# The low parts of nearly all weight units are added by accumulating transfers from HBM instead of being subtracted on GpSimd

## The chip, the cores and the metric

The kernel runs on one core of a Trainium2 chip. The metric is the device time in microseconds (us) of one execution, from its first to its last instruction. TensorE is PE, its weight loads PEld, VectorE is DVE, ScalarE is ACT, GpSimd is POOL, and SyncE is SP.

## The reference, cut to what matters

One inference step of a decoder trunk of two layers runs for 512 prompt tokens and 8 x 4 sample tokens, 544 in all, with a width of 1024 and everything in fp32. Each layer is:

```
u  = rms_norm(h, norm_mix) @ w_in                  # 25 column blocks of 128
h += concat[SSD, retention, GLA, RG-LRU](u) @ w_out # 8 column blocks
hn = rms_norm(h, norm_ffn)
h += (silu(hn @ w_gate) * (hn @ w_up)) @ w_down    # inner width 2816 = 22 blocks
```

and one last RMSNorm follows. The four mixers are recurrences in chunks with states of their own. The change touches none of them, only the way in which the weights of these products reach TensorE.

## The kernel before, in words

All weights are packed on the host into **units** of 128 partitions x 8 tiles x 128 columns, 512 KB each, 101 in a layer and 202 in all. A layer's units are, in order: 25 of w_in (numbers 0 to 24 in the layer, the mixer stage), 8 of w_out (25 to 32), then the FFN in groups: 16 gate and up units and 8 down units (33 to 56), the same again (57 to 80), and a last group of 6 blocks, REST, with 12 gate and up units (81 to 92) and 8 down units (93 to 100). A down unit of REST has only 6 tiles in use; its transfers move 8.

Each fp32 product is made of three passes over values that are split into a high and a low part: `wh*xh + wh*xl + wl*xh`. `unit_half` issues them for one unit and half of the tokens: 8 tiles x 3 matmuls of 272 columns, 48 matmuls for the two halves, 36 in a down unit of REST. `wh` is the weight rounded to fp32r by an ACT copy of `raw` (L420). `wl = raw - wh`, the **rest**, is made in one of two ways, and `added(n)` says which for unit n:

- subtracted: POOL computes `raw - wh` on 128 x 1024 (L391) as soon as `wh` is there (semaphore `lo_done`);
- added: ACT writes `wl = -raw` (L419, semaphore `negated`) ahead of `wh` (L420), and POOL issues a transfer of the unit from HBM that adds into `wl` (L397, semaphore `lo_added`). Since the destination is rounded to fp32r on both writes, what remains is the low part. ACT and the second read of the unit from HBM take the place of POOL's subtraction.

`raw`, `wh` and `wl` are rings of three slots. Unit n can be prepared only when TensorE has finished unit n-3 (`dense_done`, waited for in `hi_ahead`), so ACT's and POOL's work and the transfer must fit into the time of units n-2 and n-1. SP loads `raw` of unit n+3 (L375) when slot n is free: for an added unit after ACT's `wh` of unit n, for a subtracted one after POOL's subtraction.

ACT and DVE run their instructions in program order. In the FFN, `ffn_pair` (DVE) and `ffn_unit` (ACT) make one block of the activation: DVE scales the gate and up results (L1178), ACT takes the silu (L649), DVE multiplies (L1183), ACT rounds to the high part (L652), DVE subtracts for the low part (L1186). A group's down units need all of these, and TensorE runs the last block's matmuls of the first down unit last. In the w_out and last down units DVE adds the result to h (L1158, twice a unit), and ACT and DVE prepare the next RMSNorm (L427 squares, L431 rounds, L696 low part, L689 adds squares).

Of the kernel before, what the change touches and what calls it, by code (L numbers as in the profile page):

```python
# [60 lines left out]
NIN = len(IN_UNITS)  # L61
# [15 lines left out]
def added(n):  # L77

    layer, u = divmod(n, NUNIT)
    return (3 if layer == 0 else 1) <= u < NIN  # L80


ADDED = [sum(map(added, range(n + 1))) for n in range(ALL)]
BY_SLOT = [sum(map(added, range(n % RING, n + 1, RING))) for n in range(ALL)]


# [92 lines left out]
def trunk(nc, weights, params, consts, x, s_ssd, s_ret, s_gla, y, o_conv, o_ssd, o_ret, o_gla, o_lru,  # L179
          n_ssd, n_ret, n_gla):  # L180
    with ExitStack() as ctx:
# [173 lines left out]
        @block.sync  # L355
        def _(sp):
            sp.dma_start(raw[:, 0, :], weights[0]).then_inc(raw_loaded[0], 16)
            for i in range(KT // 2):
                sp.dma_start(h[:, 2 * i:2 * i + 2, :], x[:, 2 * i:2 * i + 2, :]).then_inc(x_loaded[i], 16)
            sp.wait_ge(x_loaded[1], 16)  # L360
            sp.dma_start(raw[:, 1, :], weights[1]).then_inc(raw_loaded[1], 16)
            sp.wait_ge(x_loaded[KT // 2 - 1], 16)
            sp.dma_start(raw[:, 2, :], weights[2]).then_inc(raw_loaded[2], 16)
            sp.dma_start(S1[:, 0:NEXACT], consts[:, NCONST + KT:NCONST + KT + NEXACT]).then_inc(exact_loaded, 16)
            sp.wait_ge(first_lo, 1)
            sp.dma_start(raw[:, 0, :], weights[3]).then_inc(raw_loaded[0], 16)
            sp.dma_start(cs[:, 0:LATE], consts[:, 0:LATE]).then_inc(consts_loaded, 16)
            sp.wait_ge(first_lo, 2)
            sp.dma_start(raw[:, 1, :], weights[4]).then_inc(raw_loaded[1], 16)
            for n in range(2, ALL - RING):  # L370
                if added(n):
                    sp.wait_ge(hi_done, n + 1)
                else:
                    sp.wait_ge(lo_done, n - 1 - ADDED[n])
                sp.dma_start(raw[:, n % RING, :], weights[n + RING]).then_inc(raw_loaded[n % RING], 16)  # L375
                if n == 6:
                    sp.dma_start(cs[:, LATE:], consts[:, LATE:NCONST]).then_inc(late_consts_loaded, 16)
            for s in range(RING):
                sp.wait_ge(raw_loaded[s], 16 * len(range(s, ALL, RING)))
            for i in range(KT // 2):  # L380
                sp.wait_ge(y_final, 2 * i + 2)
                sp.dma_start(y[:, 2 * i:2 * i + 2, :], h[:, 2 * i:2 * i + 2, :]).then_inc(y_stored, 16)
            sp.wait_ge(y_stored, 16 * (KT // 2))
            sp.wait_ge(stored, DEPTH * STORES)
# [1438 lines left out]
```

## Time and profile before

| | |
|---|---|
| three runs | 1392.46, 1392.70 and 1395.43 us, median 1392.7 |
| span of the profiled execution, and its own time | 1392.0 us, clock 0.990 |
| TensorE busy | 1361.7 us, 98% of the span |
| VectorE, ScalarE, GpSimd busy | 630.7, 492.6 and 409.9 us |
| DMA, mean over the span | 146.68 MB, 105 GB/s |

TensorE is the busy engine. Its idle time and the waits that end it are what a change away from TensorE can touch; the busy time of another engine counts only where TensorE waits for it.

### The profile page before, as it was taken

How to read it: one execution, taken by the hardware profiler on the slowest of the kernel's cores; microseconds unless marked ns; L12 is line 12 of the kernel's file. 1: busy time of each engine (PE TensorE's matmuls, PEld its weight loads, DVE VectorE, ACT ScalarE, POOL GpSimd, SP SyncE). 2: the span in 40 equal slices, each digit the busy share in tenths (PEclk: the TensorE clock that was granted, in tenths of full speed). 3: DMA queues.
4: the chain of work that ended last, by engine and by line, in shares of the span. 5: the costliest groups of instructions: out<-in, count | busy, mean ns of one | idle time of the engine just before them, and what ended most of it. 6: DMA issues, size and time to landing. Idle time of an engine off the chain costs nothing.

```text
span 1392.0 us, 26025 instructions
## 1 busy us (share of the span) xinstructions
PE 1361.7 (98%) x11309; PEld 1313.6 (94%) x11309; DVE 630.7 (45%) x1250; ACT 492.6 (35%) x675; POOL 409.9 (29%) x204
## 2 busy tenths in 40 slices
PE   7999999999999999999999999999999999999996
PEld 7888898999999999999998888899999999999996
DVE  6844765553321343133757456646443123322434
ACT  6526454432221222122553364543322122222221
POOL 1101001434433443344400100023334433443341
PEclk9999999999999999999999999999999999999998
DMA  7746633222222223222466465422222222222231
GB/s 248 182 106 154 160 80 104 89 88 81 88 91 92 83 85 91 91 87 81 130 139 156 119 156 130 106 79 90 78 91 80 89 92 92 82 86 92 91 92 65
DMA packets 42066, 146.68 MB, mean 105 GB/s; under 512 B 5216, under 2 KB 6496, under 8 KB 41952
## 3 DMA queue, kind: packets, MB, share of 16 engines
q1 hardware_dynamic: 30672, 111.95, 25.1%
q0 software_dynamic: 6624, 24.12, 10.4%
q10 hardware_dynamic: 4656, 8.95, 2.1%
q8 instruction: 89, 1.46, 0.4%
q14 instruction: 25, 0.20, 0.0%
HBM read 137.34 MB, written 5.43 MB: 103 GB/s over the span
## 4 chain that ended last, share of the span: by engine, by line
PE 85%; DVE 7%; ACT 3%; DVEq 2%; issue 1%; ACTq 1%; DMA 0%
PE bank L1261 78%; DVE ct L755 1%; PE bank L1209 1%; DVE lru_x L755 1%; PE bank L1518 1%; ACT wl L419 0%; PE bank L1524 0%; PE bank L1225 0%; DVEq L754 0%; PE bank L1220 0%; ACT wh L420 0%; DVE h L1200 0%; PE bank L1443 0%; DVE gl_gla L1186 0%; PE bank L1547 0%
## 5 line engine op out<-in xcount | busy, mean ns | idle before, releaser
L1261 PE MATMUL bank<-xh,wh 128*128 128x272 f32 x2208 | 649.8, 294 | 7.9 <-DVE xl L710 7.6
L1261 PE MATMUL bank<-xh,wl 128*128 128x272 f32 x2208 | 642.9, 291 | 0.0
L1261 PE MATMUL bank<-xl,wh 128*128 128x272 f32 x2208 | 639.3, 290 | 0.0
L391 POOL TENSOR_TENSOR wl<-raw,wh 128x1024 fp32r<-128x1024 f32 x154 | 369.7, 2400 | 591.0 <-ACT wh L420 572.1
L1261 PEld LDWEIGHTS bank<-xh,wh 128*128 128x128 f32 x2208 | 420.0, 190 | 19.4 <-issue 17.5
L420 ACT ACTIVATE wh<-raw 128x1024 fp32r<-128x1024 f32 x199 | 210.2, 1056 | 611.3 <-PE bank L1261 611.3
L1261 PEld LDWEIGHTS bank<-xl,wh 128*128 128x128 f32 x2208 | 420.5, 190 | 1.0 <-issue 1.0
L1261 PEld LDWEIGHTS bank<-xh,wl 128*128 128x128 f32 x2208 | 419.3, 190 | 0.0
L1178 DVE TENSOR_TENSOR tz<-bank,rs_bcast 128x272 f32<-128x272 f32 x176 | 77.6, 442 | 293.3 <-PE bank L1261 289.3
L1158 DVE TENSOR_TENSOR h<-h,bank 128x272 f32<-128x272 f32 x128 | 55.4, 436 | 217.3 <-PE bank L1261 217.2
L397 POOL DMA_DIRECT2D wl<-weights x46 | 40.0, 870 | 365.2 <-ACT wl L419 365.2
L419 ACT ACTIVATE wl<-raw 128x1024 fp32r<-128x1024 f32 x46 | 48.5, 1054 | 88.8 <-PE bank L1261 76.8
L1261 PE MATMUL bank<-gh_gla,wh 128*128 128x272 f32 x256 | 73.9, 289 | 1.0 <-DVE gl_gla L1186 1.0
L1261 PE MATMUL bank<-gh_ret,wh 128*128 128x272 f32 x256 | 74.3, 290 | 0.0
L1261 PE MATMUL bank<-gl_ret,wh 128*128 128x272 f32 x256 | 74.0, 289 | 0.0
L1261 PE MATMUL bank<-gh_ssd,wh 128*128 128x272 f32 x256 | 74.0, 289 | 0.0
L1261 PE MATMUL bank<-gh_ssd,wl 128*128 128x272 f32 x256 | 73.9, 289 | 0.0
L1261 PE MATMUL bank<-gh_ret,wl 128*128 128x272 f32 x256 | 73.8, 288 | 0.0
L1261 PE MATMUL bank<-gh_gla,wl 128*128 128x272 f32 x256 | 73.8, 288 | 0.0
L1261 PE MATMUL bank<-gl_ssd,wh 128*128 128x272 f32 x256 | 73.3, 286 | 0.0
L1261 PE MATMUL bank<-gl_gla,wh 128*128 128x272 f32 x256 | 73.2, 286 | 0.0
L689 DVE TENSOR_TENSOR sq_sum<-sq_sum,Vx 128x544 f32<-128x544 f32 x30 | 54.0, 1801 | 3.6 <-issue 1.3
(360 smaller groups left out, 1721.1 us busy)
## 6 DMA issues: line engine op xcount, KB each, us to landing
raw<-weights SPq DMA_DIRECT2D x202, 512.0 KB, 3.6
wl<-weights POOLq DMA_DIRECT2D x46, 512.0 KB, 6.9
h<-x SPq DMA_DIRECT2D x4, 544.0 KB, 6.0
y<-h SPq DMA_DIRECT2D x4, 544.0 KB, 2.7
rv<-rk ACTq DMA_DIRECT2D x8, 136.0 KB, 4.0
tz<-rq ACTq DMA_DIRECT2D x8, 136.0 KB, 5.4
S<-s_ssd ACTq DMA_DIRECT2D x2, 512.0 KB, 7.0
n_ssd<-Vx ACTq DMA_DIRECT2D x2, 512.0 KB, 2.8
```

Of the source, the lines that this page charges most:

```text
L391: nc.gpsimd.tensor_tensor(wl[:, s, :], raw[:, s, :], wh[:, s, :].bitcast(F32), ALU.subtract).then_inc(lo_done, 1)
L397: nc.gpsimd.dma_start(wl[:, n % RING, :], weights[n], accum_op=ALU.add).then_inc(lo_added[n % RING], 16)
L419: a(wl[:, s, :], raw[:, s, :], ACT.Copy, scale=-1.0).then_inc(negated, 1)
L420: a(wh[:, s, :], raw[:, s, :], ACT.Copy).then_inc(hi_done, 1)
L689: tt(sq_sum[:], sq_sum[:], sq[:, m % 2, :], ALU.add).then_inc(sq_added.sem, 1)
L755: ins = stt(out, row[:, j:j + CW], par(layer, w, 4 * (t % 4) + j), out, ALU.mult, ALU.add)
L1158: ins = tt(h[:, m, cols], h[:, m, cols], acc, ALU.add)
L1178: tt(tz[:, i // 2, cols], acc, rs_bcast[:, cols], ALU.mult).then_inc(dense_free.sem, 1)
L1209: return nc.tensor.transpose(out, src, exact("ident", n_in, 0, n_in).bitcast(F32))
L1261: ins = mm(bank_, wt[:, n % RING, w], xx[:, cols], start=(i == 0 and j == 0), stop=(i == len(ks) - 1 and j == 2))
L1518: ins = mm(M[4][0:n, at:at + 2], sq[:, t, off:off + n], cst("pair"), start=True, stop=True)
```

## The change

`added` is true for units 3 and up of layer 0 and for all but the first unit of layer 1, where before it was true up to unit 24 of each layer (the w_in units). So the rests of w_out and of the whole FFN, 76 units a layer and 152 in all, are added by transfers. Added units go from 46 to 198, subtracted ones on POOL from 154 to 2. `ADDED` and `BY_SLOT`, the counts that semaphores are compared with, follow from `added`.

```diff
 def added(n):
 
     layer, u = divmod(n, NUNIT)
-    return (3 if layer == 0 else 1) <= u < NIN
+    return u >= 3 if layer == 0 else u != 0
```

On ACT, at the end of REST's gate and up units and the start of its down units in layer 0 (`gh_gla` is the high part of an activation block here, `h_new` and `act_out` come from DVE), before:

```order
L420 ACTIVATE wh<-raw 128x1024 [waits dense_done,raw_loaded2]
L652 ACTIVATE gh_gla<-tz 128x544 [waits act_out]
L420 ACTIVATE wh<-raw 128x1024 [waits dense_done,raw_loaded0]
L427 ACTIVATE sq_sum<-h 128x544 [waits h_new]
L431 ACTIVATE xh<-h,pr 128x544
L420 ACTIVATE wh<-raw 128x1024 [waits dense_done,raw_loaded1]
```

and now:

```order
L419 ACTIVATE wl<-raw 128x1024 [waits dense_done,raw_loaded2]
L420 ACTIVATE wh<-raw 128x1024
L652 ACTIVATE gh_gla<-tz 128x544 [waits act_out]
L419 ACTIVATE wl<-raw 128x1024 [waits dense_done,raw_loaded0]
L420 ACTIVATE wh<-raw 128x1024
L427 ACTIVATE sq_sum<-h 128x544 [waits h_new]
L431 ACTIVATE xh<-h,pr 128x544
L419 ACTIVATE wl<-raw 128x1024 [waits dense_done,raw_loaded1]
L420 ACTIVATE wh<-raw 128x1024
```

One negation stands ahead of each `wh`, and with it ahead of the rounding L652 and of the squares.

On POOL, the whole program after its constants, before and now:

```order
L391 TENSOR_TENSOR wl<-raw,wh 128x1024 [waits hi_done]
L397 DMA wl<-weights 128x1024 [waits negated] x22
L391 TENSOR_TENSOR wl<-raw,wh 128x1024 [waits hi_done] x77
L397 DMA wl<-weights 128x1024 [waits negated] x24
L391 TENSOR_TENSOR wl<-raw,wh 128x1024 [waits hi_done] x76
```

```order
L391 TENSOR_TENSOR wl<-raw,wh 128x1024 [waits hi_done]
L397 DMA wl<-weights 128x1024 [waits negated] x98
L391 TENSOR_TENSOR wl<-raw,wh 128x1024 [waits hi_done]
L397 DMA wl<-weights 128x1024 [waits negated] x100
```

152 subtractions have become issues of transfers. SP's loads of `raw` behind them now wait for `hi_done` in place of `lo_done`. The instructions on TensorE and VectorE are the same, in the same order; TensorE's first matmul of a unit waits for `hi_done` and `lo_added` where it waited for `lo_done`.

## Rows read from the trace of the kernel before

**Rows 1.** The page: span, busy times, costliest groups (busy us, mean ns | idle before).

```profile
span 1392.0 us, 26025 instructions
PE 1361.7 (98%) x11309; PEld 1313.6 (94%) x11309; DVE 630.7 (45%) x1250; ACT 492.6 (35%) x675; POOL 409.9 (29%) x204
...
L391 POOL TENSOR_TENSOR wl<-raw,wh 128x1024 fp32r<-128x1024 f32 x154 | 369.7, 2400 | 591.0 <-ACT wh L420 572.1
```

**Rows 2.** Waits of TensorE, whole span: us in total, times, longest.

```profile
PE bank L1220 <- DVE sq_sum L689: 1.5, 1, 1.5
...
PE bank L1261 <- DVE gl_gla L1186: 1.0, 2, 0.5
```

**Rows 3.** Timeline at the REST boundary of layer 0, 656.5 to 661.

```profile
656.71 1.06 ACT L420 ACTIVATE wh<-raw 128x1024 fp32r<-128x1024 f32 x1 [4.43 <-PE bank L1261]
...
657.95 0.66 ACT L652 ACTIVATE gh_gla<-tz 128x544 fp32r<-128x544 f32 x1 [0.17 <-DVE tz L1183]
...
658.64 2.19 DVE L1186 TENSOR_TENSOR gl_gla<-tz,gh_gla 128x544 fp32r<-128x544 f32 x1 [0.72 <-ACT gh_gla L652]
...
660.09 0.29 PE L1261 MATMUL bank<-gh_gla,wl 128*128 128x272 f32 x1
...
660.89 0.39 PE L1261 MATMUL bank<-gh_gla,wh 128*128 128x272 f32 x1 [0.51 <-DVE gl_gla L1186]
```

**Rows 4.** L1186, the FFN's low parts: ns min/median/max.

```profile
L1186 DVE TENSOR_TENSOR gl_gla<-tz,gh_gla x12: 2190/2191/2195, 356.8 to 1341.3; 128x544 fp32r<-128x544 f32 x12
```

**Rows 5.** L1084, the mixers' low parts, same operation and shape.

```profile
L1084 DVE TENSOR_TENSOR gl_gla<-tz,gh_gla x4: 726/726/726, 223.6 to 911.5; 128x544 fp32r<-128x544 f32 x4
```

**Rows 6.** Timeline of an added unit: negation, `wh`, issue.

```profile
689.15 1.06 ACT L419 ACTIVATE wl<-raw 128x1024 fp32r<-128x1024 f32 x1 [2.28 <-PE bank L1261]
...
690.12 1.04 ACT L420 ACTIVATE wh<-raw 128x1024 fp32r<-128x1024 f32 x1
690.51 0.88 POOL L397 DMA_DIRECT2D wl<-weights  x1 [2.33 <-ACT wl L419]
```

**Rows 7.** Line L397, whole span: issue to landing of 46 transfers.

```profile
DMA to landing us min/median/max: 6.5/6.9/9.6
```

**Rows 8.** The same, 706 to 722: two issues 6.0 us apart.

```profile
L397 POOL DMA_DIRECT2D wl<-weights x2: 865/865/865, 710.1 to 716.2; - x2
...
DMA to landing us min/median/max: 6.8/6.8/6.9
```

**Rows 9.** The same, 690 to 700: two issues 4.5 us apart.

```profile
L397 POOL DMA_DIRECT2D wl<-weights x2: 865/871/877, 690.5 to 695.0; - x2
...
DMA to landing us min/median/max: 7.3/7.7/8.1
```

**Rows 10.** Timeline, a down unit of REST from end to end.

```profile
666.46 0.44 DVE L1158 TENSOR_TENSOR h<-h,bank 128x272 f32<-128x272 f32 x1 [1.82 <-PE bank L1261]
666.52 1.06 ACT L420 ACTIVATE wh<-raw 128x1024 fp32r<-128x1024 f32 x1 [2.28 <-PE bank L1261]
...
670.99 0.44 DVE L1158 TENSOR_TENSOR h<-h,bank 128x272 f32<-128x272 f32 x1 [1.82 <-PE bank L1261]
```

**Rows 11.** Stages: span, busy us of PE, PEld, DVE, ACT, POOL; clock, DMA share, GB/s.

```profile
75.96:106.51 30.55, 30.55 (x266) 27.15 (x266) 14.15 (x40) 8.44 (x16) 2.59 (x3) 1.00 0.47 104
...
400.00:450.00 50.00, 50.00 (x400) 50.00 (x399) 7.44 (x17) 9.02 (x9) 19.83 (x9) 1.00 0.29 86
```

**Rows 12.** Timeline at the first w_out units, layer 0.

```profile
246.45 1.04 ACT L420 ACTIVATE wh<-raw 128x1024 fp32r<-128x1024 f32 x1
...
249.10 0.44 DVE L1158 TENSOR_TENSOR h<-h,bank 128x272 f32<-128x272 f32 x1 [0.32 <-PE bank L1261]
...
255.14 0.44 DVE L1158 TENSOR_TENSOR h<-h,bank 128x272 f32<-128x272 f32 x1 [2.56 <-PE bank L1261]
```

**Rows 13.** The same place in layer 1.

```profile
929.12 1.04 ACT L420 ACTIVATE wh<-raw 128x1024 fp32r<-128x1024 f32 x1
...
937.80 0.44 DVE L1158 TENSOR_TENSOR h<-h,bank 128x272 f32<-128x272 f32 x1 [2.56 <-PE bank L1261]
```

## The prediction

> **What bounds the kernel now.** I read the page first, then TensorE's waits, then the stages, then single places. The page says that TensorE is busy for 98% of the span and GpSimd for 410 us, of which 370 are the 154 subtractions [rows 1]. A busy GpSimd costs nothing if nobody waits for it, and the view of waits says that TensorE does not: no wait of it in the whole span is ended by GpSimd or by a `wl` [rows 2]. In the stages that the change touches (w_out and FFN, about 243 to 697 and 925 to 1392) TensorE waits twice for the low part `gl_gla` of L1186, once a layer, and then only in the tail, after the last matmul of the last unit [rows 2]. In the middle of the FFN it is busy for 50 of 50 us at full clock [rows 11]. A unit of 8 tiles takes 255.14 - 249.10 = 6.04 us [rows 12], or 6.04/48 = 0.126 us a matmul; a down unit of REST, with 6 tiles, 670.99 - 666.46 = 4.53 us [rows 10].
>
> So the change can win only what those two waits hold, and it can lose wherever a transfer lands later than a subtraction was done.
>
> **What it removes.** 152 subtractions of 2.40 us [rows 1]. As such they are worth nothing. They do slow VectorE: L1186 takes 2.19 us in the FFN, where each one meets a subtraction on GpSimd [rows 3, 4], and the same operation on the same shape takes 0.73 us in the mixer stage, where GpSimd does not compute [rows 5]. TensorE waits for just this at the REST boundary: the matmul at 660.89 should have started at 660.09 + 0.126 = 660.215, so 0.675 us are lost [rows 3]; layer 1 has the same wait [rows 2]. The chain there is: ACT's `wh` at 656.71, L652 at 657.95, L1186 from 658.64 to 660.83 [rows 3]. Now ACT first negates. A negation moves the next ACT instruction by 690.12 - 689.15 = 0.97 us [rows 6], so `wh` starts at 657.68, L652 at 658.65, L1186 at 658.65 + 0.69 = 659.34, and it ends 0.73 us later at 660.07, 0.15 us ahead of its need. The waits go: **-0.675 x 2 = -1.35 us**. If L1186 stayed at 2.19 us, the later L652 would make the wait 0.70 us longer instead, +1.4 us for both; I exclude it, since nothing computes on GpSimd then.
>
> **What it adds on ScalarE.** 152 negations of 1.06 us. In the fullest stretch, the down units, ACT stands idle for 2.28 us ahead of each `wh` [rows 10]. A negation takes 0.97 of it and leaves 1.3 us, so ACT stays ahead of TensorE: 0. Without that cover each unit would come up to 0.97 us later.
>
> **What it adds on the transfers' side.** 152 reads more of 512 KB, and TensorE now waits for each to land. The chain for unit n begins when TensorE ends unit n-3. ACT's negation starts 0.06 us later [rows 10], the issue stands 690.51 - 689.15 = 1.36 us behind the negation's start [rows 6], and the landing comes L behind the issue. L was 6.5 to 9.6 us, median 6.9 [rows 7]. Unit n starts two units after unit n-3 ended. With 0.1 us for handing over:
>
> - Units of 8 tiles: 2 x 6.04 - 1.42 - 0.1, so L may be 10.5 us. Even the longest of 46, 9.6, is in time. Two issues 6 us apart, each with its `raw` load, landed in 6.8 and 6.9 us [rows 8]. Cost 0, with 3.6 us to spare over the median.
> - Down units of REST: 2 x 4.53 - 1.52 gives an L of 7.5 us. Six units a layer have two short units ahead of them.
> - The third w_out unit. ACT comes to its weights late, at 246.45, and TensorE wants it at 255.14 [rows 12]: 8.69 - 1.36 - 0.1 gives an L of 7.2 us. In layer 1, 937.80 - 929.12 gives the same 7.2 [rows 13].
>
> How large does L get? One added unit moves `raw` and the adding transfer. Three of them fill 0.47 of 30.55 us of all DMA engines, 4.79 us each [rows 11]; `raw` alone fills 0.29 of 6.04 us, 1.75. In the 8-tile units 4.79 of 6.04 us fits. In the down units 4.79 us of work come every 4.53 us, so a queue builds: 0.26 us a unit, behind a first overlap of 0.3 us. I take that overlap from the two issues 4.5 us apart, which landed in 8.1 and 7.3 us [rows 9]: the lower one is 0.4 over the median. I take 6.9, 7.2, 7.45, 7.7, 8.0, 8.2 us for the six units. Unit n's issue hangs on unit n-3, mostly one that was not yet late, so these delays do not add up; what counts is the largest excess, 8.2 - 7.5 = **0.7 us in layer 0**. In layer 1 the last three units have no `raw` load beside them, so the queue ends at 7.7: **0.2 us**. At the third w_out unit I take 7.4 in layer 0, where the program also loads parameters (L637), **0.2 us**, and 6.9 in layer 1, 0.
>
> Bounds of these three: with every L at 6.9 they are 0; with every L at 9.6, each down group loses (9.6 - 7.5) x 2 = 4.2 us (an excess comes back once, three units on) and each w_out stage 2.4, 13.2 us in all. I stay near the low end, because Rows 9 is the nearest row and its mean is 7.7.
>
> The page "DMA: Bandwidth & Descriptors" of the Trainium skill, section "Anatomy of one DMA — SWDGE (gpsimd) path", fits a GpSimd-issued transfer at 2.0 us + bytes/436e3, an estimate of 3.2 us for 512 KB. By it no transfer would ever be late and the sum would be -1.35 us alone. This case's trace has 6.5 us as its shortest, so the trace decides against it for adding transfers.
>
> SP's loads of `raw` no longer wait behind a subtraction, so they are issued earlier, and they have three units to land in: 0. The tail has no GpSimd work in it: 0.
>
> **The sum.** -1.35 + 0.7 + 0.2 + 0.2 = -0.25 us against the profiled execution's 1392.0, so 1391.8. The median of the runs is 0.7 above that execution: **1392.4 us**. A measurement here tells about 0.2%, 2.8 us, from no change, so this is "the same".
>
> **The rivals.**
>
> *The transfers are late (slower).* The adding transfers saturate the DMA engines in the down units and crowd the two close issues at the third w_out unit. The loss is 2 x 2 x (L - 7.5) + 2 x (L - 7.2) - 1.35. It passes 2.8 us from a sustained L of 8.1 on. At 8.7 us it is 4.8 + 3.0 - 1.35 = +6.5: 1399 us. For it: 8.1 us was seen once in rows 9, and 4.79 is above 4.53. Against it: the excess lasts six units only. The same page of the skill, section "Issuing engines are not separate DMA queues", says that transfers from all engines end on the same 16 DMA engines and interleave; that is the mechanism here, and the DMA shares of rows 11 agree. Chance 0.18.
>
> *All transfers are hidden (the change away from VectorE's delay is all that shows).* L stays at 6.9 to 7.2: -1.35, so 1391.3 us. For it: a queue of 0.26 us a unit may drown in the spread. Chance 0.10, within 0.2%.
>
> *Faster by over 0.2%.* The two waits hold 1.35 us together, and the other stalls of these stages lie in the tail. A gain of 2.8 us would need something that this trace doesn't show. Chance 0.04.
>
> My forecast, a small gain eaten by small lateness, has 0.68. Within 0.2%: 0.68 + 0.10 = 0.78; slower 0.18; faster 0.04. The range goes from 1390.8 (all hidden, and half a microsecond of spread) to 1397.5, which leaves out the upper half of the first rival.
>
> **What would show it.** L1186 at 0.73 us everywhere, and TensorE's waits for it gone. 198 transfers, of which the ones in the 8-tile units land in 6.5 to 7.5 us, and the last ones of each layer in 7.5 to 8.2. New waits of TensorE at the down units and at the third w_out unit, under 1 us each. DMA share near 0.8 in the middle of the FFN against 0.29, with TensorE still at 50 of 50 us there. It would be wrong if landings in the 8-tile units passed 10.5 us, if TensorE's matmuls came less densely than 0.126 us apart beside the transfers, or if the down units waited 2 us or more.

## The result, and the profile after

The changed kernel took 1397.4 us (median of 11 runs, 1395.1 to 1403.0), the kernel before in the same series 1393.7 us (11 runs, 1392.5 to 1395.5). The ratio is 1.003, with a 95% interval of 1.0019 to 1.0041: slower by 0.3%, which is 4.2 us between the means and 3.7 us between the medians. The time lies in the range of the prediction, but near its upper end, and the prediction was "the same", a quarter of a microsecond under before; "slower" had 0.18.

The page of the changed kernel; the lines answer to [rows 1]:

```profile
span 1393.3 us, 26189 instructions
PE 1362.8 (98%) x11309; PEld 1314.3 (94%) x11309; DVE 537.2 (39%) x1250; ACT 631.7 (45%) x827; POOL 176.1 (13%) x204
...
HBM read 217.03 MB, written 5.43 MB: 160 GB/s over the span
...
L419 ACT ACTIVATE wl<-raw 128x1024 fp32r<-128x1024 f32 x198 | 209.6, 1059 | 577.4 <-PE bank L1261 565.3
...
L397 POOL DMA_DIRECT2D wl<-weights x198 | 171.2, 865 | 1166.6 <-ACT wl L419 1134.9
```

GpSimd went from 409.9 to 176.1 us and VectorE from 630.7 to 537.2; ScalarE rose from 492.6 to 631.7. TensorE, which bounds the kernel, stayed at 98%. This execution took 1395.08 us, the shortest of the eleven, so its profile shows less than the usual loss. Three more profiles of the same kernel are therefore read below (experiments 1, 10 and 11).

L1186, the answer to [rows 4], and L689 in a stretch of the w_out and first FFN units; over the whole span its median was 2739 ns in the kernel before:

```profile
L1186 DVE TENSOR_TENSOR gl_gla<-tz,gh_gla x12: 724/726/726, 357.7 to 1342.4; 128x544 fp32r<-128x544 f32 x12
```

```profile
L689 DVE TENSOR_TENSOR sq_sum<-sq_sum,Vx x6: 724/726/727, 262.9 to 293.0; 128x544 f32<-128x544 f32 x6
```

The REST boundary of layer 0, the answer to [rows 3]:

```profile
656.94 1.06 ACT L419 ACTIVATE wl<-raw 128x1024 fp32r<-128x1024 f32 x1 [3.48 <-PE bank L1261]
...
657.90 1.04 ACT L420 ACTIVATE wh<-raw 128x1024 fp32r<-128x1024 f32 x1
...
658.85 0.64 ACT L652 ACTIVATE gh_gla<-tz 128x544 fp32r<-128x544 f32 x1
...
659.52 0.73 DVE L1186 TENSOR_TENSOR gl_gla<-tz,gh_gla 128x544 fp32r<-128x544 f32 x1 [1.39 <-ACT gh_gla L652]
...
660.57 0.29 PE L1261 MATMUL bank<-gl_gla,wh 128*128 128x272 f32 x1
```

The chain runs as predicted: negation, `wh`, L652, and L1186 ends at 660.25, ahead of the low part's matmul. The row of waits for L1186 [rows 2] is gone. In its place stands one for the transfers. TensorE's waits in the changed kernel, whole span (us in total, times, longest):

```profile
PE bank L1220 <- DVE sq_sum L689: 1.8, 2, 1.5
...
PE bank L1261 <- DMA wl<-weights: 0.9, 3, 0.3
```

Issue to landing of L397 in layer 0: first 66 transfers of 8-tile units (256 to 655 us), then the 6 of REST's down units (656 to 689 us).

```profile
L397 POOL DMA_DIRECT2D wl<-weights x66: 862/862/883, 256.8 to 652.2; - x66
...
DMA to landing us min/median/max: 6.6/6.9/8.9
```

```profile
L397 POOL DMA_DIRECT2D wl<-weights x6: 862/864/865, 658.3 to 681.9; - x6
...
DMA to landing us min/median/max: 6.8/7.2/8.2
```

In the units of 8 tiles even the longest, 8.9 us, is far from the 10.5 us that they allow (65 more in layer 1 give 6.6/6.9/9.1; the longest in the other three profiles is 9.3). In the down units 8.2 is past the allowed 7.5. The windows say why (us, busy us of PE, PEld, DVE, ACT, POOL; clock, DMA share, GB/s); the first answers to [rows 11], the second is the down units of layer 0.

```profile
400.00:450.00 50.00, 50.00 (x400) 50.00 (x399) 7.45 (x17) 16.61 (x17) 6.90 (x8) 1.00 0.78 172
```

```profile
656.00:684.00 28.00, 27.48 (x217) 27.10 (x216) 11.97 (x21) 18.53 (x23) 5.18 (x6) 1.00 0.93 218
```

At a DMA share of 0.78 TensorE is busy for 50 of 50 us. In the down units the DMA engines are at 0.93, and TensorE is idle for 0.52 of 28 us.

### The profile page after: what moved, and what is told of

The parts are those of the page before. It is cut to its first block, busy times and chain, and to the rows that moved or that the text cites. A ratio compares the mean times of both kernels' runs of the same rounds, so it can differ in the third digit from the quotient of the medians.

```text
span 1393.3 us, 26189 instructions
## 1 busy us (share of the span) xinstructions
PE 1362.8 (98%) x11309; PEld 1314.3 (94%) x11309; DVE 537.2 (39%) x1250; ACT 631.7 (45%) x827; POOL 176.1 (13%) x204
## 4 chain that ended last, share of the span: by engine, by line
PE 83%; DVE 7%; ACT 3%; DVEq 2%; DMA 2%; issue 1%; ACTq 1%; SPq 0%
PE bank L1261 76%; DVE ct L755 1%; DMA wl<-weights 1%; PE bank L1209 1%; DVE lru_x L755 1%; ACT wl L419 1%; PE bank L1518 1%; PE bank L1225 0%; PE bank L1524 0%; DMA h<-x 0%; DVEq L754 0%; PE bank L1220 0%; DVE sq_sum L689 0%; ACT wh L420 0%; DVE h L1200 0%
## 5 line engine op out<-in xcount | busy, mean ns | idle before, releaser
L419 ACT ACTIVATE wl<-raw 128x1024 fp32r<-128x1024 f32 x198 | 209.6, 1059 | 577.4 <-PE bank L1261 565.3
L397 POOL DMA_DIRECT2D wl<-weights x198 | 171.2, 865 | 1166.6 <-ACT wl L419 1134.9
L1158 DVE TENSOR_TENSOR h<-h,bank 128x272 f32<-128x272 f32 x128 | 55.7, 438 | 247.4 <-PE bank L1261 247.3
L1261 PE MATMUL bank<-gl_lru,wh 128*128 128x272 f32 x192 | 55.5, 289 | 0.0
L1261 PE MATMUL bank<-gh_lru,wh 128*128 128x272 f32 x192 | 55.4, 289 | 0.0
```

What stands on the lines that cost most here:

```text
L397: nc.gpsimd.dma_start(wl[:, n % RING, :], weights[n], accum_op=ALU.add).then_inc(lo_added[n % RING], 16)
L419: a(wl[:, s, :], raw[:, s, :], ACT.Copy, scale=-1.0).then_inc(negated, 1)
L1158: ins = tt(h[:, m, cols], h[:, m, cols], acc, ALU.add)
L1261: ins = mm(bank_, wt[:, n % RING, w], xx[:, cols], start=(i == 0 and j == 0), stop=(i == len(ks) - 1 and j == 2))
```

## The experiments

Three theories were tested. **A**, the first rival of the prediction: the loss is made by transfers that land late, in the 16 down units of REST and perhaps at the third w_out unit. **B**: the loss is made by the extra traffic and ScalarE work of all the other units, without a wait that a profile shows. **C**: the waits are small, and stretches of TensorE at its lower clock that follow them carry most of the time. Each edit stands against the changed kernel. Ratios are to the kernel before, run on the same chip; the brackets are 95% intervals.

### 1. The changed kernel again, unedited (e1_repeat)

> The changed kernel again, unedited. Known: 1397.4 us median of 11 runs, scattered from 1395.1 to 1403.0, where the kernel before scatters from 1392.5 to 1395.5. Theory A (little slack in two places: landings that scatter beyond 7.5 us in the down units of REST and 7.2 us at the third w_out unit): the median is again 3 to 4 us over before, and a profile shows the waits for wl in these places alone. Theory B (a long tail: single landings of over 10.5 us in the 8-tile units, where a landing is tolerated up to that): the waits for wl lie anywhere in the FFN, few and long, 1 us or more each. Theory C (TensorE's clock): the waits themselves are small, and stretches at half clock that follow them carry most of the time; executions that take longer have a lower mean clock.

Measured: 1398.1 us (12 runs, 1394.7 to 1400.8), ratio 1.0023 (1.0011 to 1.0034). The slowdown came again in this second series. Its profiled execution is a more usual one, 1398.9 us. It shows a late transfer as a chain. On GpSimd the issues of the down units stand 4.5 us apart until one is late:

```profile
662.08 0.86 POOL L397 DMA_DIRECT2D wl<-weights  x1 [3.64 <-ACT wl L419]
666.61 0.86 POOL L397 DMA_DIRECT2D wl<-weights  x1 [3.66 <-ACT wl L419]
671.14 0.86 POOL L397 DMA_DIRECT2D wl<-weights  x1 [3.67 <-ACT wl L419]
675.94 0.86 POOL L397 DMA_DIRECT2D wl<-weights  x1 [3.94 <-ACT wl L419]
```

and on TensorE the first matmul of the unit whose transfer was issued at 666.61 comes 1.28 us late:

```profile
675.78 0.37 PE L1261 MATMUL bank<-gh_ssd,wh 128*128 128x272 f32 x1 [1.28 <-DMA wl<-weights]
```

The landings of this stretch:

```profile
DMA to landing us min/median/max: 6.7/7.4/9.0
```

The longest, 9.0 us, is 1.5 over the allowed 7.5. It belongs to the unit just named, the fifth down unit (number 97). A second wait of 1.0 us stands in the down units of layer 1, where the prediction had 0.2. The 1.28 + 1.0 us are less than the 4 us that are to be explained, so I looked for where else time goes.

The profile shows a second kind of loss. At the end of layer 0 TensorE runs the norm's sum as 20 matmuls of one column (L1220, L1225), and right behind them its clock falls. Timeline of the repeat:

```profile
697.86 0.96 PE L1225 MATMUL bank<-ones,Vx 128*128 128x1 f32 x8
...
699.35 0.29 PE L1261 MATMUL bank<-xl,wh 128*128 128x272 f32 x1
...
699.48 0.29 PE L1261 MATMUL bank<-xh,wl 128*128 128x272 f32 x1
...
700.45 0.43 PE L1261 MATMUL bank<-xl,wh 128*128 128x272 f32 x1
...
700.68 0.43 PE L1261 MATMUL bank<-xh,wl 128*128 128x272 f32 x1
```

Matmuls that started 0.125 us apart start 0.227 us apart for 3.4 us: the lower of the two clock levels, 1.2 instead of 2.4 GHz. The window around it, first in the repeat and then in the changed kernel's own profile:

```profile
696.00:706.00 10.00, 10.00 (x70) 9.73 (x70) 3.10 (x9) 4.06 (x7) 0.44 (x1) 0.83 0.62 148
```

```profile
696.00:706.00 10.00, 10.00 (x83) 9.73 (x82) 3.00 (x9) 4.82 (x7) 1.21 (x2) 1.00 0.62 143
```

Thirteen matmuls fewer in 10 us are 13 x 0.125 = 1.6 us. The page "TensorE: Matmul & The Clock Gate" of the Trainium skill, section "What's actually happening", says that the clock follows how busy TensorE has been recently, and that the number of slow matmuls at the start of one kernel changes from run to run. The fall behind a block of one-column matmuls would agree with the first; that the same block is followed by it in one profile and not in another is the same kind of scatter, in the middle of a kernel. That one kernel should show it more often than the other is not explained there.

Each run also lists its span and mean granted clock. Span times (1 - clock) estimates what the lower clock took, and the rest holds the waits. It is a rough split, because the tail, where TensorE mostly waits, also runs at the lower clock. Means over all runs, with one standard error ("before" is from the repeat's series, on one chip; the 11 runs of the changed kernel are from the first series, whose runs of before list no clock):

| | span | by the clock | rest |
|---|---|---|---|
| before (35 runs) | 1392.97 | 15.05 ± 0.36 | 1377.92 ± 0.11 |
| changed (11 runs) | 1396.47 | 16.89 ± 0.62 | 1379.59 ± 0.31 |
| the repeat (12 runs) | 1396.18 | 16.76 ± 0.52 | 1379.43 ± 0.32 |

So of 3.5 us of span (3.2 in the repeat) some 1.6 lie in the rest and some 1.8 in the clock (an estimate: the clocks are listed to a thousandth, which is 1.4 us in a single run). The two halves are questions of their own. Which stages the waits lie in is told in the part on why the prediction was wrong.

### 2. Six tiles instead of eight in the down units (e2_six_tiles)

```diff
+def tiles_of(n):
+    return (REST if n % NUNIT >= REST0 + 2 * REST else KT) * P
...
-nc.gpsimd.dma_start(wl[:, n % RING, :], weights[n], accum_op=ALU.add)
+nc.gpsimd.dma_start(wl[:, n % RING, 0:w], weights[n][:, 0:w], accum_op=ALU.add)
```

The load of `raw`, the negation and `wh` are cut to the same 6 tiles, the ones that a down unit of REST uses.

> The changed kernel, but in the down units of REST all four steps (load of raw, negation, wh, adding transfer) move only the 6 tiles that are used instead of 8. The DMA work of such a unit falls from 4.8 to 3.6 us, under its period of 4.53, and a landing should come 1 us earlier. Theory A: at least two thirds of the loss goes, the median is 0.5 to 1.5 us over before or lower, waits for wl only at the third w_out unit. Theory B: nothing changes, 1396.5 to 1398. Theory C: like A, since the waits that pull the clock down go.

Measured: 1395.8 us, ratio 1.0003 (0.9992 to 1.0014); by the medians 1.5 us over before, at the edge of what A expected. The down units of layer 0:

```profile
656.00:684.00 28.00, 28.00 (x225) 28.00 (x224) 11.91 (x21) 15.27 (x23) 5.17 (x6) 1.00 0.87 172
```

TensorE is busy for 28 of 28 us, and the landings end at 7.4 us, within 7.5. With 4.79 x 6/8 = 3.6 us of transfer work for every 4.53 us (an estimate) the loss of layer 0's down units goes. What was left for `wl` in its profile was 0.3 us once at the third w_out unit, and 0.6 us at the fifth down unit of layer 1. The profile puts this second wait down to VectorE's L1164 (here the line of L1158), but that result had been there long before, and the adding transfer of the unit, issued at 1353.0, took 8.3 us and landed 0.14 us before the matmul at 1361.43. Its clock fell at 700 us as in the repeat (0.83), behind down units without any wait; that goes against C, by which the waits bring the fall on.

### 3. The down units from the fourth on subtracted (e3_down_sub)

```diff
-    return u >= 3 if layer == 0 else u != 0
+    return u < 96 and (u >= 3 if layer == 0 else u != 0)
```

> The changed kernel, but the last five down units of REST of each layer (96 to 100) are subtracted on GpSimd as before. Units 3 to 95 stay added, so the REST boundary keeps VectorE's gain of 1.35 us. Theory A: no wait for wl is left in the down units; the median falls to that of before or up to 1 us under it, 1393 to 1395, what is left being the third w_out unit. Theory B: it stays at 1396 to 1398, since 8-tile units keep their adding transfers.

Measured: 1393.3 us, ratio 0.9991 (0.9978 to 1.0004). The 142 other changed units cost nothing that shows, against B. The last added unit, 95, still waits 0.8 us once, in layer 0, though A expected no wait: its transfer, with the usual 6 us to the one before, took 8.2 us.

### 4. The FFN up to unit 95 alone (e4_deep_only)

```diff
+    return u < 96 and not OUT0 <= u < FFN0 and (u >= 3 if layer == 0 else u != 0)
```

> As the one with the last five down units subtracted, but the eight w_out units are subtracted too, so that of the 152 changed units only the 63 a layer with at least 12 us of slack stay added. Theory A: no wait for wl is left, the median is 1 us under before (1392 to 1393.5). Theory B: 1395.5 or more, because these 126 units have the same rare late landings. This is the kernel that tells A from B.

Measured: 1394.8 us, ratio 1.0001 (0.9991 to 1.0011), no wait for a `wl`. Together with the third kernel this refutes B: 126 added units, with a DMA share of 0.75 from 256 to 655 us, cost nothing that can be measured. The stages of the profiles say it more sharply. From the first matmul of a stage to the first of the next, the second group's gate and up units take 96.63 us, REST's gate and up units 72.47 us and each group of eight full down units 48.26 us, to within 0.02 us in both layers of all 14 profiles, whether the rests are added or subtracted. A had expected 1392 to 1393.5 us, and that did not come. In the trace the gain at the REST boundary is there in full (see the seventh kernel); over the runs the rest, as in the table above, fell by 0.7 ± 0.3 us only, and why by no more stays open.

### 5. `raw` loaded behind the adding transfer (e5_raw_after)

```diff
+                    if n % NUNIT >= OUT0:
+                        sp.wait_ge(lo_added[n % RING], 16 * BY_SLOT[n])
```

It sits ahead of SP's load of `raw` for unit n+3, so that the two transfers don't run beside each other.

> The changed kernel, but from the first w_out unit on SP loads raw of unit n+3 only when the adding transfer of unit n has landed, so the two are not queued side by side from the start. The same bytes and the same number of transfers. Theory A (the down units wait for landings that share the DMA engines with raw): an adding transfer without a raw load beside it landed in 5.4 to 5.5 us, so landings in the 8-tile units fall from 6.9 to 5.5 to 6.3 us, in the down units under 7.5; the waits for wl there fall to under 0.5 us a layer and the median comes to within 1 us of before. If the number of bytes or of transfers costs by itself, the time stays at 1397 to 1398.

Measured: 1396.6 us, ratio 1.0012 (1.0000 to 1.0025), about half of the loss, and not the return to within 1 us of before that A expected. In the 8-tile units of the FFN (405 to 640 us) the landings are 5.2/6.7/8.1 us, with a median far above the 5.5 to 6.3 expected. Its profile still has two waits for `wl` of 0.8 us in the down units of layer 0, and there

```profile
DMA to landing us min/median/max: 5.6/6.8/8.5
```

The shortest fell from 6.8 to 5.6 us, the longest did not fall. Reordering the same bytes doesn't mend a stretch in which 4.79 us of work come every 4.53 us; the second kernel, with fewer bytes, did so in layer 0.

### 6. Only the 16 down units added (e6_down_added)

```diff
+    return (3 if layer == 0 else 1) <= u < NIN or u >= 93
```

> The complement of the kernel that added the deep units only: besides the w_in units, which were added before, only the eight down units of REST of each layer (93 to 100) are added, 16 units in place of 152. Theory A: nearly the whole loss comes back with these 16 units, 2.5 to 4 us over before. Theory B or a cost of each transfer: 16 of 152 transfers give a tenth of the loss, 0 to 0.5 us, less the gain of 1.35 us at the REST boundary, so it would be under before.

Measured: 1399.8 us (5 runs, 1398.6 to 1401.0), ratio 1.0030 (1.0019 to 1.0042). Sixteen of the 152 converted units bring the whole loss, by this median 5.1 us over before, more than the 2.5 to 4 that A expected. In the profile TensorE waits for `wl` longer than in any other:

```profile
PE bank L1261 <- DMA wl<-weights: 2.8, 4, 0.9
...
PE bank L1261 <- DVE h L1158: 0.5, 1, 0.5
```

```profile
656.00:684.00 28.00, 26.25 (x206) 25.68 (x204) 11.51 (x20) 17.60 (x22) 5.18 (x6) 1.00 0.91 212
```

The second row is a late transfer too, by the same reading as in the second kernel: the unit's own transfer landed 0.14 us before the matmul. Here the units ahead were subtracted and the DMA engines fairly idle, and still the six landings took 7.7 to 9.1 us. So the queue doesn't come in from the units before; it is made within the group. In layer 1 of this kernel the six took 6.6, 7.5, 8.4, 6.3, 5.5 and 5.7 us, as in the changed kernel.

### 7. Only the unit whose subtraction meets L1186 (e7_one_unit)

```diff
+    return (3 if layer == 0 else 1) <= u < NIN or u == 95
```

> The kernel before with a single further added unit in each layer, number 95, whose subtraction is the one that meets L1186 at the REST boundary. This is VectorE's gain alone: TensorE's two waits for L1186 go, 1.35 us less than before, 1392.5 to 1393.5 where before has 1394. If the gain of 1.35 us were an error of the timeline, it would be the same as before or slower.

Measured: 1393.8 us against 1394.7, ratio 0.9990 (0.9981 to 0.9999): the only kernel whose whole interval lies below 1. GpSimd is free where TensorE waited for VectorE, and L1186 takes

```profile
661.59 0.72 DVE L1186 TENSOR_TENSOR gl_gla<-tz,gh_gla 128x544 fp32r<-128x544 f32 x1 [1.39 <-ACT gh_gla L652]
```

while the other low parts of the FFN stay at 2190 ns. No wait for L1186 or for a `wl` is left. The rest (as in the table above) is 1376.5 ± 0.4 against 1377.7, 1.2 us less (± 0.4), where the prediction had 1.35. The trace is sharper: REST's down units take 36.20 us in layer 0 for 36.97 before, and 36.07 for 36.85 in layer 1, so 1.55 us go. The 0.2 us over the prediction are the matmul behind each waiting one, which starts 0.11 us late as well. That term holds.

### 8. The kernel before, as one of the series (e8_before_again)

> The kernel before, once more as a kernel of its own, for a second profile. It should be the same within 0.1%. What is asked is where its stretches at half clock lie: theory C says that the changed kernel has about one more of them in an execution on average, because its waits come shortly ahead of the norm at a layer's end; the repeat of the changed kernel had two that the first profile of before has not, at 700 and 983 us. If this profile has stretches at such places too, they are scatter that both kernels share.

Measured: 1394.7 us, ratio 0.9996 (0.9987 to 1.0004). It shows what such a comparison gives without any change: 0.04% or 0.6 us, with an interval of ±0.09%. Its profile has two stretches at the lower clock of the same kind, at 234 and at 299 us, and none at 700. So such stretches belong to both kernels; whether one at 700 is more frequent in the changed one is the question of the last three profiles.

### 9. Six tiles, and the third w_out unit subtracted (e9_six_and_27)

The edits of the second kernel, and

```diff
+    return u != 27 and (u >= 3 if layer == 0 else u != 0)
```

> The changed kernel with both narrow places eased: the down units of REST move 6 tiles instead of 8 in all four steps, and the third w_out unit (27) is subtracted on GpSimd. All other rests, 196 of them, are added. Theory A: nothing of the loss is left and VectorE's gain shows, 1.35 us under before by the waits, so 1393 to 1394 where before has 1394.5; a part of the scatter in the clock may stay. If the 150 further transfers cost something by themselves, it stays 1 us or more over before.

Measured: 1394.8 us, ratio 1.0002 (0.9992 to 1.0012). A expected the full gain of 1.35 us here, and it did not come. Its profile has one wait for `wl`, 0.8 us, in the down units of layer 1, where the landings were

```profile
DMA to landing us min/median/max: 4.8/5.9/8.5
```

A median of 5.9 and one of 8.5: even at six tiles one transfer a layer can be late. It is again the fifth down unit's, as in the second kernel (8.3 us), and in layer 1 alone; in layer 0 this unit's took 6.2 and 6.3 us. Why it is late there stays open. It takes 1.0 of the 1.55 us in this execution; the remainder is within the uncertainty.

### 10 to 12. Three more profiles (e10_changed_look, e11_changed_look, e12_before_look)

The changed kernel twice and the kernel before once, one execution each, to see whether the clock's fall at 700 us goes with the changed kernel.

> The changed kernel, one more profile. Of the five profiles so far of kernels that add all down units of REST, four have a stretch at half clock right behind the 20 one-column matmuls of the norm at the end of layer 0 (about 700 us); of the five that do not add them all, none has. If the waits in the down units bring it on, it should be here again in most looks, and the waits for wl in the two down groups should sum to 1.5 to 3 us.

> The changed kernel, a further profile, with the same question: a stretch at half clock near 700 us, yes or no, and the sum of the waits in the down groups, 1.5 to 3 us.

> The kernel before, a third profile. No stretch at half clock near 700 us if that one hangs on the changed down units; one there would say that it is scatter which both kernels share.

Measured: 1396.6, 1399.1 and 1393.8 us. The same window, in this order:

```profile
696.00:706.00 10.00, 10.00 (x70) 9.72 (x69) 3.27 (x9) 4.02 (x6) 0.61 (x1) 0.83 0.62 151
```

```profile
696.00:706.00 10.00, 10.00 (x76) 9.94 (x75) 3.45 (x8) 5.56 (x8) 0.86 (x1) 0.89 0.91 194
```

```profile
696.00:706.00 10.00, 10.00 (x81) 9.73 (x81) 3.27 (x11) 3.91 (x5) 0.86 (x1) 1.00 0.62 131
```

(In the second the stretch starts at 703.9, and the window cuts it.) Over all profiles: the fall at 700 us is in six of the eight of kernels that add all down units of REST (the changed kernel's repeat and these two profiles, the second, fifth and sixth kernel; not in the changed kernel's first profile and not in the ninth), and in none of the six of the others (before three times, the third, fourth and seventh). The waits for `wl` in the two profiles are 1.3 and 2.4 us in all. Of the 2.4 us, 1.4 lie in the down units, with 0.6 more behind a late transfer that the profile puts down to L1158; so the down groups have 1.3 and 2.0 us for the expected 1.5 to 3. The other 1.1 us are a wait at the third w_out unit of layer 0:

```profile
256.85 0.36 PE L1261 MATMUL bank<-gh_ssd,wh 128*128 128x272 f32 x1 [1.09 <-DMA wl<-weights]
```

## Why the prediction was wrong

**What held.** L1186 at 0.73 us, both of its waits gone, with a gain of 1.55 us in the trace and 1.2 ± 0.4 over the runs, for 1.35. ScalarE's negations cost nothing that shows. The 8-tile units cost nothing, with landings of 6.6 to 9.1 us for an allowed 10.5 and TensorE at 50 of 50 us. The DMA share there was 0.78 for "near 0.8". The place of the loss was right, too: new waits in the down units, each of 0.2 to 1.3 us. And so was the rule that the late units do not add up: in each group the loss is the largest landing less what is allowed, plus 0.08 us for the matmul behind; in one group of eight a second unit (99) came late as well.

**The step that failed: "I take 6.9, 7.2, 7.45, 7.7, 8.0, 8.2 us for the six units".** Issue to landing by unit, means of the four profiles of the changed kernel:

| unit | 95 | 96 | 97 | 98 | 99 | 100 |
|---|---|---|---|---|---|---|
| predicted, layer 0 | 6.9 | 7.2 | 7.45 | 7.7 | 8.0 | 8.2 |
| measured, layer 0 | 6.8 | 7.6 | 8.6 | 7.8 | 7.5 | 6.8 |
| measured, layer 1 | 6.7 | 7.6 | 8.4 | 6.4 | 5.4 | 5.5 |

The prediction let the queue grow by 0.26 us a unit, the work less the period, and reach its longest at the end. It grew by 0.9 us a unit over the first two steps and was longest at unit 97, the third of the six, in both layers and in all four profiles, but for one tie with unit 99: 8.2, 9.0, 8.6 and 8.5 us in layer 0, 8.2, 8.8, 8.2 and 8.6 in layer 1. Behind it the late unit itself puts the next issues further apart, and the landings fall. So the last three units of layer 1 have no `raw` load beside them, as I had said, but the longest transfer comes before them, and layer 1 loses nearly as much as layer 0. Why the transfers grow by 0.9 and not by 0.26 us, no run shows.

A smaller part is the limit. The issue came 1.59 us behind the end of unit n-3 (for 1.42), and the matmul 0.14 us behind the landing (for 0.1), so 7.3 us were allowed and not 7.5.

How much it cost, from the first matmul of REST's down units to the first behind them (in layer 1 to their last):

| us | layer 0 | layer 1 |
|---|---|---|
| before | 36.97 | 36.85 |
| no late transfer and no wait for L1186 (experiments 4 and 7) | 36.20 | 36.07 |
| changed, four profiles | 37.19, 38.00, 37.54, 37.98 | 37.01, 37.59, 37.06, 37.46 |

Against the second row the late transfers cost 1.5 us in layer 0, predicted 0.7, and 1.2 us in layer 1, predicted 0.2. [Rows 9] could have warned: there the first of two close transfers took 8.1 us and the second 7.3, so the lower one, which I took for the start of a queue, was not its start.

**The third w_out unit**, predicted 0.2 us in layer 0, waited in one of the four profiles, where its transfer took 8.3 us for an allowed 7.0 and the stage came out 1.33 us longer; in the others it took 6.7 to 6.9 us. That is 0.3 us on average, from a single case. In the second kernel it waited once, for 0.3.

**The sum** with the measured terms is -1.55 + 1.5 + 1.2 + 0.3 = about +1.5 us where it had -0.25. The rest by the table is +1.6 ± 0.3, so within these errors the waits account for it.

**A term that was missing: TensorE's clock.** By the same table some 1.8 us (± 0.7) of the difference lie in it, and the prediction had nothing for it. What the profiles show is a 3.4 us stretch at the lower level behind the one-column matmuls of the norm that follows REST's down units, 1.6 us each time; at six times in eight that is 1.2 of the 1.8. It goes with adding all down units, six of eight against none of six, and this is a correlation; the place was chosen after the first profiles, and only the last three asked about it in advance. The size is no firmer: the fifth kernel has the stretch too, and its part by the clock is 15.5 ± 0.7 us against 15.3 ± 0.4 before. A wait in the down units is not needed to bring it on, since the second kernel had the stretch in layer 0 without any such wait there. DMA share in the window doesn't tell it apart either: 0.62 with it and without it. The cause is open, and with it about half of the slowdown.

**The rival.** "The transfers are late" named the right mechanism and place, but as a sustained L of 8.7 us in all six units and at w_out. What came was one peak a group, 8.4 to 8.6 us on average, and the clock made up the size: that the time comes near this rival's 1399 us is in part luck. With the slack of 7.5 us so near the median of 6.9 and a row of 9.6 in the trace, it deserved more than 0.18.

**The baseline.** The kernel before ran at 1393.7 to 1394.7 us where the three runs shown had 1392.7. An execution's time was 1.8 us above its span in the changed kernel (1395.08 against 1393.3) and 2.0 in the kernel before, so the metric holds more than the span, and I had put the median only 0.7 above 1392.0. So forecast and range both started 1 to 2 us too low. The ratio doesn't depend on it.

## What to carry to other kernels

Where a transfer replaces work on an engine, compare its allowed time, at the shortest units that wait for it, with the longest landings in the trace and not with their median; where the DMA work of a unit exceeds the unit's own time, look for fewer bytes first: here they removed the loss in one layer, and a new order of the same bytes halved it. Convert the piece of work that somebody waits for, and leave the rest: one unit a layer gave the whole gain (0.1%), and the sixteen down units of REST, this one among them, the whole loss (0.3%). A profile of one execution can be a lucky one; compare its time with the median of its runs before its waits are taken for the loss. And where a stage has a length that repeats to 0.01 us, its length measures a loss better than the list of waits, which leaves out small ones and can name the wrong releaser.

## What the runs showed of the hardware

- In the changed kernel's profile adding transfers of 512 KB landed in 6.6 to 9.1 us at one even spacing of 6 us (131 transfers, median 6.9), each with a `raw` load of the same size beside it. Issued every 4.5 us, the first three took 6.8, 7.6 and 8.6 us (layer 0, means of four profiles). At the end of layer 1, where no `raw` load stands beside them, the shortest took 5.2 to 5.5 us.
- VectorE's 128x544 fp32 subtraction (L1186) takes 2187 to 2195 ns where GpSimd subtracts beside it and 724 to 727 ns where it doesn't, with nothing between in any profile here.
- Behind a block of one-column matmuls TensorE ran at its lower clock for 3.4 us in some executions and in others not, with the same instructions. The stretch at 700 us was always behind such a block. Others came at 299 us in profiles of both kernels, at 234 us in one of before and one of the second kernel, and at 983 us in one of the changed kernel, besides two in layer 1's mixer stage, near 857 and 881 us, that nearly all profiles have.
